# Hybrid decoder layer: the causal mask of the softmax scores moved from a TensorE matmul into VectorE's row-maximum pass

## The reference, cut to what matters

```
s_sel = where(m_sel, (q @ k_sel) * scale, NEG_INF);  p = softmax(s_sel);  o_sel = p @ v_sel
s_win = where(m_win, (q @ k_win) * scale, NEG_INF);  p = softmax(s_win);  o_win = p @ v_win
s_own = where(k_pos <= q_pos, (q @ k) * scale, NEG_INF);  ...      # MoBA, together with the earlier block
```

## Time and profile before

| | |
|---|---|
| median of 3 runs | 636.16 us (635.68 to 637.22) |
| profiled execution, own time | 636.81 us |
| its span in the trace | 635.0 us |
| TensorE busy | 606.6 us (96%) |
| VectorE busy | 386.8 us (61%) |
| ScalarE busy | 302.1 us (48%) |
| GpSimd busy | 247.4 us (39%) |
| mean granted clock of TensorE | 0.99 of full speed |

### The profile page before, as it was taken

The page is one execution under the profiler, slowest core; times in us unless marked ns, Lnnn a source line. Parts: engine busy times, 40 slices in busy tenths (PEclk is TensorE's granted clock), DMA queues, the critical chain, the costliest instruction groups (busy, mean ns, idle before and its releaser), DMA issues.

```text
span 635.0 us, 8412 instructions
## 1 busy us (share of the span) xinstructions
PE 606.6 (96%) x3172; PEld 499.2 (79%) x3172; DVE 386.8 (61%) x665; ACT 302.1 (48%) x541; POOL 247.4 (39%) x120
## 2 busy tenths in 40 slices
PE   2999999999989989999999999999999999999995
PEld 2988888886876667889987888888888888888884
DVE  4526031104878877288499968569577595681656
ACT  5415264107566974255563564425545445453422
POOL 4422527402526351005336564172533723812611
PEclk9999999999989989999999999999999999999999
DMA  9442449513240222002704353250340613203002
GB/s 281 136 132 68 132 117 233 127 40 116 85 133 10 59 82 85 1 1 67 266 1 165 101 170 96 76 190 2 133 133 2 211 55 132 67 1 126 40 34 100
DMA packets 45724, 63.50 MB, mean 100 GB/s; under 512 B 6616, under 2 KB 34292, under 8 KB 45684
## 3 DMA queue, kind: packets, MB, share of 16 engines
q1 hardware_dynamic: 45524, 62.71, 32.0%
q10 hardware_dynamic: 160, 0.26, 0.2%
HBM read 58.51 MB, written 2.10 MB: 95 GB/s over the span
## 4 chain that ended last, share of the span: by engine, by line
PE 89%; DVE 5%; ACT 2%; issue 1%; DMA 1%; POOL 1%; SPq 0%; DVEq 0%; ACTq 0%
PE ps L1616 20%; PE ps L1617 19%; PE ps L1618 19%; PE ps L2006 7%; PE ps L2008 7%; PE ps L2007 7%; PE ps L1878 2%; PE ps L1758 1%; PE ps L1863 1%; DMA raw<-in_w_in 1%; PE ps L1782 1%; PE ps L1783 1%; DVE stat L1290 1%; DVE probsT L1302 1%; PE ps L1934 1%
## 5 line engine op out<-in xcount | busy, mean ns | idle before, releaser
L1618 PE MATMUL ps<-xT_h,ring_l 128*128 128x512 f32 (+1 forms) x384 | 143.1, 373 | 0.0
L1616 PE MATMUL ps<-xT_h,ring_h 128*128 128x512 f32 (+1 forms) x384 | 143.0, 372 | 0.0
L1617 PE MATMUL ps<-xT_l,ring_h 128*128 128x512 f32 (+1 forms) x384 | 143.0, 372 | 0.0
L661 POOL TENSOR_TENSOR ring_l<-raw_d,ring_h 128x1024 fp32r<-128x1024 f32 x25 | 67.4, 2707 | 130.8 <-ACT ring_h L931 130.8
L661 POOL TENSOR_TENSOR ring_l<-raw,ring_h 128x1024 fp32r<-128x1024 f32 x31 | 76.8, 2502 | 83.9 <-DVE xres L1459 44.4
L604 POOL TENSOR_TENSOR ring_l<-raw,ring_h 128x2048 fp32r<-128x2048 f32 (+1 forms) x16 | 69.5, 4353 | 85.6 <-ACT ring_h L679 85.6
L1553 DVE TENSOR_TENSOR y<-ps,y 128x512 f32<-128x512 f32 x90 | 61.2, 688 | 52.6 <-PE ps L2008 52.2
L1616 PEld LDWEIGHTS ps<-xT_h,ring_h 128*128 128x128 f32 x384 | 72.6, 189 | 12.9
L1617 PEld LDWEIGHTS ps<-xT_l,ring_h 128*128 128x128 f32 x384 | 72.3, 188 | 12.6
L1618 PEld LDWEIGHTS ps<-xT_h,ring_l 128*128 128x128 f32 x384 | 72.3, 188 | 12.6
L2006 PE MATMUL ps<-ring_h,a_h 128*128 128x512 f32 x196 | 77.4, 395 | 0.0
(11 more groups left out here) (248 smaller groups left out, 995.5 us busy)
## 6 DMA issues: line engine op xcount, KB each, us to landing
raw<-in_w_mlp SPq DMA_DIRECT2D x16, 1024.0 KB, 5.4
raw_d<-in_w_mlp SPq DMA_DIRECT2D x16, 1024.0 KB, 6.0
raw<-in_w_in SPq DMA_DIRECT2D x9, 1024.0 KB, 5.3
raw<-in_nsa_cmp_w SPq DMA_DIRECT2D x8, 512.0 KB, 7.2
xres<-in_x SPq DMA_DIRECT2D x4, 512.0 KB, 5.9
raw<-in_w_out SPq DMA_DIRECT2D x2, 1024.0 KB, 6.4
raw<-in_w_out SPq DMA_DIRECT2D x4, 512.0 KB, 4.3
out<-xres SPq DMA_DIRECT2D x8, 256.0 KB, 2.1
```

What stands on the lines that cost most here:

```text
L661: nc.gpsimd.tensor_tensor(slot(ring_l, n), slot_source(n), slot(ring_h, n).bitcast(F32), ALU.subtract).then_inc(lo_done, 1)
L1616: nc.tensor.matmul(o, sh, mh, start=start, stop=False)
L1617: nc.tensor.matmul(o, sh, ml, start=False, stop=False)
L1618: return nc.tensor.matmul(o, sl, mh, start=False, stop=stop)
```

## The change

The mask matmul L1784 is left out. The mask becomes a tile of 128x512 bf16 of which the last 128 columns hold the triangle and the others zeros, so that its last `w` columns fit a score of width `w`. The row maximum is now one instruction that reads the scores from PSUM and the mask, writes the negative of their sum over the scores in PSUM, and gives the minimum of that as its accumulator output, which is the negative row maximum as before. The exponential takes its input with a scale of -1. A small tile (`a21`) moves to the place of the old constants. On TensorE both scores of a unit now stand ahead of `back`, `values` and both heads' transposes.

```
-        mask_s = put("mask_s", [P, P], BF16)
+        mask_s = put("mask_s", [P, SEQ], BF16)
...
-        a21 = at("a21", [P, TH], F32, o_m + 49152)
+        a21 = at("a21", [P, TH], F32, o_dead)
...
-            nc.gpsimd.affine_select(out=mask_s[:], in_=mask_s[:], compare_op=ALU.is_ge, fill=NEG, base=0,
+            nc.gpsimd.affine_select(out=mask_s[:, SEQ - P:SEQ], in_=mask_s[:, SEQ - P:SEQ], compare_op=ALU.is_ge, fill=NEG, base=0,
...
-                nc.scalar.activation(probs[:, s % 3, 0:w], ps[:, S_BANK[s % 5], 0:w], ACT.Exp,
+                nc.scalar.activation(probs[:, s % 3, 0:w], ps[:, S_BANK[s % 5], 0:w], ACT.Exp, scale=-1.0,
...
-                nc.vector.tensor_reduce(stat[:, NMAX + s:NMAX + s + 1], ps[:, S_BANK[s % 5], 0:w], AX.X, ALU.max,
-                                        negate=True).then_inc(mx_done, 1)
+                scores = ps[:, S_BANK[s % 5], 0:w]
+                nc.vector.tensor_tensor_reduce(scores, scores, mask_s[:, SEQ - w:SEQ], -1.0, 3e38, ALU.add, ALU.min,
+                                               stat[:, NMAX + s:NMAX + s + 1]).then_inc(mx_done, 1)
...
-                nc.tensor.matmul(ps[:, bank, 0:n], q[:, i * P:(i + 1) * P], kl[:, 0:n], start=False, stop=True)
-                nc.tensor.matmul(ps[:, bank, w - P:w], identb[:], mask_s[:], start=False,
-                                 stop=True, skip_group_check=True).then_inc(s_done, 1)
+                nc.tensor.matmul(ps[:, bank, 0:n], q[:, i * P:(i + 1) * P], kl[:, 0:n], start=False, stop=True).then_inc(s_done, 1)
...
-                for m in range(2):
-                    s = 2 * u + m
-                    if s + 4 < 2 * NU:
-                        score(s + 4)
-                    if m == 0 and g and i == 3:
-                        back(g - 1)
-                    if m == 0 and g and i == 1:
-                        values(g - 1)
+                for s in (2 * u + 4, 2 * u + 5):
+                    if s < 2 * NU:
+                        score(s)
+                if g and i == 3:
+                    back(g - 1)
+                if g and i == 1:
+                    values(g - 1)
+                for s in (2 * u, 2 * u + 1):
                     transposes(s)
```

More of the change, by code:

```diff
@@ L268, in build @@
         gained = at("gained", [P, 2, SEQ], F32, o_m + 45056)
-        assert o_dead <= o_a - 8192, (o_dead, o_a)
-        assert o_r + 6144 <= nc.sbuf_usable_end and o_m + 50176 <= nc.sbuf_usable_end, (o_r + 6144, nc.sbuf_usable_end)
+        assert o_dead + 1024 <= o_a - 8192, (o_dead, o_a)
+        assert o_r + 6144 <= nc.sbuf_usable_end and o_m + 49152 <= nc.sbuf_usable_end, (o_r + 6144, nc.sbuf_usable_end)
         ps = ctx.enter_context(nc.psum_tensor("ps", [P, 8, 512], F32))
@@ L1912, in _ @@
                         cmp_out(CO_S.index(s))
[L1913 to L1916, removed]
+                if u == NU - 2:
+                    pe.wait_ge(ml_y, 2)
+                    y_transposes(0)
+                    y_transposes(1)
             def project(t, half, k_lo, k_hi):
```

## The result

The kernel after takes 640.24 us, the median of 7 runs (637.81 to 640.53), the kernel before in the same job 635.68 (634.51 to 637.22, 7 runs). The ratio is 1.0062, with a 95% interval of 1.0046 to 1.0078: 0.6% slower. The forecast was 637.3 with a range of 634.2 to 641.0. The time is in the range, on the slow side, and above the likeliest case's own range (636.3 to 638.4).

The account below looks back on a forecast made before the run. Three engines coupled by waits were taken as the bound: TensorE busy 53.0, VectorE 47.8, ScalarE 47.0 of the stage's 58.27 us. Path terms of +1.0 and +0.1 summed to +1.1 us on the 636.16 median: 637.3, range 634.2 to 641.0.

Parts of the forecast that it names:

- To 202.56: Stage up to the first value product: masks saved, score 11 moved ahead, transposes overlapping less; -0.2 us.
- 202.56 to 212.13: Second stretch of the path: value product starts at 203.5, behind the extra score, `exp(21)` at 206.2; +0.7 us.
- 212.13 to 219.57: Next stretch: value product at 213.4, its exponential +1.2 us, 0.3 given back; copy L679 0.85 to 0.9 us later.
- To 228.33: Fifth stretch: L679 and GpSimd's L604 end 0.85 us later, two row maxima add 2 x 0.09; sum +1.0 us.
- hidden: Value product near 223.4: its first transposes done at 226.1, before L604 ends at 227.0, so their delay costs nothing.
- To 241.32: Last stretch: value product at 232.88 comes 1.0 us later, replacing the earlier 1.0; one more row maximum adds 0.1 us.
- The new row maximum: VectorE: main part unchanged, accumulator read 0.09 us each (bounds 0 and 0.19), 4.1 us for 46 in the six stretches.
- The mask matmul: TensorE: 48 removed at 0.07 us each, 3.4 us at full clock; only what lies in full stretches can show.
- The clock: Rival: new wait near 221 drops TensorE to 1.2 GHz, +1 to +1.7 us; chance 0.25, shared with dearer VectorE.
- the dearer case: Rival: VectorE's accumulator read costs 0.19 us (638.5), or the clock falls once more (638.5 to 639.5); chance 0.25.
- The slow instruction: Rival: VectorE's new row maximum runs at half rate, 9 us or more added, 646 to 650 us; chance 0.08.
- TensorE's saving as the net effect: Rival: no value product waits for the extra score, so removed masks show: 632.8 to 635.1 us; chance 0.17.

Follow-up runs that it names:

- e2: The kernel before with only the new loop order; mask matmul and plain row maximum stay: 638.68 us, ratio 1.0047.
- e1: The kernel after with the old loop order, so only the mask moves to VectorE: 635.32 us, ratio 0.9996 to the kernel before.
- e5: The kernel after with no mask at all and the plain row maximum, scores not causal: 638.53 us, ratio 1.0049 to the kernel before.
- e7: e1 plus eight idle 256-column matmuls in TensorE's longest wait, ahead of the transposes of score 38: 634.45 us, ratio 0.9985 to the kernel before.
- e8: e1 with ScalarE's weight copy L679 one unit earlier: 633.58 us, ratio 0.9966 to the kernel before.
- e10: The kernel before with only ScalarE's weight copy L679 one unit earlier: 635.33 us, ratio 0.9999.
- e11: The kernel after with ScalarE's weight copy L679 one unit earlier: 637.71 us, ratio 1.0039 to the kernel before.

## Why the prediction came out as it did

It is taken step by step, all from the two profiles; the predicted starts of the value products were 203.5, 213.4, 223.4, 233.9 (232.88 + 1.0) and 242.4.

- *"To 202.56":* right. 203.93 was measured; 0.33 of the 0.4 us beyond 203.5 arose ahead of the stage, which starts at 183.38 instead of 183.05.
- *"202.56 to 212.13":* predicted 9.9 us, measured 11.84, of which 1.7 are the low clock in the value product at 203.93; 0.24 are path. The mechanism (value product behind the score, `exp(21)` late) is there, row for row.
- *"212.13 to 219.57" and "To 228.33":* the value product was to come 10.0 us after the last; it came 10.37 after it (10.44 in e2). L679 started at 223.06, 3.5 after its old place instead of 0.85 to 0.9. 1.7 of that are the low clock ahead of it, 0.33 what came before the stage; some 0.6 remain.
- *"hidden":* this word is where the sum was too small. The prediction has the value product 2.7 us late where the fifth stretch begins and 1.0 late where it ends; it let 1.7 us vanish in a stretch with 1.93 us of wait and 1.7 us of low clock. They did vanish in this pair of profiles: the stretch took 10.50 us, 10.48 were predicted. That agreement is luck. It was not the wait that took them up but the low clock, which stayed away from this stretch: 12.21 - 1.7 = 10.5 is what the kernel before would need there at full clock (e1 needs 10.66). Nor is the path the predicted one, behind GpSimd's L604: L1355 takes 0.20 us and stalls nobody. ScalarE waits 1.85 us for the transposes behind the value product, and from 228.98 works almost without a gap (L679 at 233.56 among it) until the exponential at 235.36 frees the bank for which TensorE waits 1.40 us, to 235.97. Against a full clock nothing is hidden: e2 has +0.8, +0.9, +2.1 and -0.2 beside e1, and the medians give 638.68 - 635.24 = 3.4 us for the new order, where the forecast's sum for everything was 1.1.
- *"To 241.32":* 8.28 us between the last two value products, 8.5 predicted.
- *The new row maximum:* the accumulator read was sized at 0.09 us. By the slots it is 0.05 (0.65 us, against 0.6 before by the prediction's own rate for two row maxima), and the main part 710 ns for 512 elements in the mean (684 before). Both were paid in time that nothing waited for (e5). The rule of the Trainium skill ("VectorE: DVE Perf Modes", section "Two Vector instructions with no wait between them") that an accumulator output makes two instructions is what the trace shows, at 142 ns for the second.
- *The mask matmul:* 0.07 us each held (from the second matmul of a 256-wide score to the transposes behind it 0.12 us in e1, 0.19 before); 1.3 to 1.5 of the 3.4 us reach the end at equal clock. That only what lies in full stretches can show is confirmed, though more of it shows than the 1.1 us of the two full stretches.
- *The clock* was a rival: one more fall to 1.2 GHz with a value product in it, +1 to +1.7 us, up to 639.5. It came, in the profile at the first wait of this kind and not at the one near 221 that was named; 5 of 7 runs have a mean clock as low as the profile's or lower. In the profiles the low stretch within the stage only changed places, from the fifth stretch to the third; ahead of the stage the kernel before has two more in its profile and the kernel after one, at 166 to 169 us. Since most runs of the kernel before have about one low stretch less than its profile (0.994 against 0.990), it counts against the median all the same.
- *The base:* the profiled execution of before was taken as 0.65 us above the median. That of after is 0.16 above its own. It is 0.5 us of the difference.

Together: 637.9 was predicted for the profile and 640.40 measured, +2.5: 0.33 ahead of the stage, 1.7 clock, 0.5 path. The order as the cause, the engines that wait, and the places where they do were right, but not the path from the fourth value product on. The term that was too small is that of the new order: the whole sum is +1.1 us, while at full clock the stage is 59.8 us long instead of some 56.6. It looked small because the later value product was taken as hidden behind L604, in a stretch that was long by its low clock. That the result still lies in the range is owed to the range, which goes up to 641.0 for the dearer case and the clock; the measured loss is four times the forecast's. The slow instruction, the stall behind GpSimd, and TensorE's saving as the net effect didn't come.

What stays open is why the clock falls where it does. The two kernels with TensorE's longest wait cut to 1.1 us and no new order keep it up (e7 in 9 of 12 runs, e8 in 5 of 5). But the kernel before has a wait of 1.9 us in its profile and keeps it up in 25 of 33 runs, e10 waits 0.9 us at most for an exponential and is at 0.988 in 4 of 12, and e11 waits as the kernel after does (4.3 us in total, 4.6 there) and is at 637.2 to 638.0 in 6 of 7. The link between work, waits and clock is observed across kernels here; no run isolates it.

## What to carry to other kernels

Work of an in-order engine that needs nothing belongs ahead of the instruction that has to wait, not behind it: there it fills the wait, while behind it the partner engine waits it out in turn. A change of two halves is to be run as halves; here one half is neutral, the other costs 3.4 us, together they cost 4.6, and with one more edit (e8) the neutral half is a gain of 0.3%. Medians of kernels with different clocks can hide a cost: compare runs of one clock, and the length of the stage at full clock. And before a stall in a profile is counted as cover, compare the profile's mean clock with those of the timed runs: cover that only some executions have hides nothing in the median.

## What the runs showed of the hardware

- An in-place pass of VectorE over PSUM, read and written in the same bank with a second operand in SBUF, ran at nearly the rate of a plain row maximum: 710 against 684 ns for 128x512, at most 735, also beside GpSimd's operation of 4.55 us (the pass at 225.36 takes 0.73). Its accumulator read lasts 142 ns, and the instruction behind starts together with it.
- Idle matmuls may make a kernel faster. e7 does eight matmuls more than e1 and is 0.9 us faster in the median, 634.45 against 635.32 in different jobs, the runs of both between 633.3 and 636.8, with 9 of 12 runs at clock 0.994 or more instead of 1 of 12. The Trainium skill ("TensorE: Matmul & The Clock Gate", section "What's actually happening") has activity as what releases the clock; e7 agrees, while e11 shows that the time waited is not all of it.
